# Position bias of a decoder layer: one scratch copy read as reversed, paced skewed blocks

## What is computed

```python
def t5_bucket(dist):
    max_exact = NUM_BUCKETS // 2
    n = jnp.maximum(dist, 0)
    nf = jnp.maximum(n, max_exact).astype(jnp.float32)
    large = max_exact + (jnp.log(nf / max_exact) / math.log(MAX_DISTANCE / max_exact)
                         * (NUM_BUCKETS - max_exact)).astype(jnp.int32)
    large = jnp.minimum(large, NUM_BUCKETS - 1)
    return jnp.where(n < max_exact, n, large)
...
        bias = bias_tab[t5_bucket(t_pos[None, :, None] - sel)]
        logits = logits + jnp.moveaxis(bias, 3, 2)
        logits = jnp.where(valid[:, :, None, :], logits, -jnp.inf)
        p = jax.nn.softmax(logits, axis=-1)
```

## Time and profile before

| | |
|---|---|
| median of 3 runs | 2173.0 us |
| lowest, highest | 2170.37, 2174.82 us |
| span of the profiled execution | 2173.1 us |
| TensorE matmul busy | 2142.9 us, 99% |
| VectorE busy | 1208.3 us, 56% |
| ScalarE busy | 962.8 us, 44% |
| GpSimd busy | 31.4 us, 1% |
| mean HBM rate | 188 GB/s |

### The profile page before, as it was taken

The page is one execution under the profiler, slowest core; times in us unless marked ns, Lnnn a source line. Parts: engine busy times, 40 slices in busy tenths (PEclk is TensorE's granted clock), DMA queues, the critical chain, the costliest instruction groups (busy, mean ns, idle before and its releaser), DMA issues.

```text
span 2173.1 us, 25372 instructions
## 1 busy us (share of the span) xinstructions
PE 2142.9 (99%) x9610; PEld 1769.4 (81%) x9610; DVE 1208.3 (56%) x1419; ACT 962.8 (44%) x1079; POOL 31.4 (1%) x57
## 2 busy tenths in 40 slices
PE   8999999999999999799999999999999999999998
PEld 7888888888888887688888888888888888888887
DVE  5545445444444656699577655465545445444444
ACT  5444444444444453344465444464444444444442
POOL 0000000000000000200000000000000000000000
PEclk9999999999999999899999999999999999999999
DMA  7666666665666566666555566656666666666664
GB/s 233 211 188 189 187 192 189 187 190 187 194 193 193 172 184 169 178 205 185 167 162 181 174 192 209 187 187 199 192 187 190 186 191 190 186 189 194 193 193 151
DMA packets 213607, 408.76 MB, mean 188 GB/s; under 512 B 17361, under 2 KB 17689, under 8 KB 213152
## 3 DMA queue, kind: packets, MB, share of 16 engines
q1 hardware_dynamic: 208752, 399.16, 60.6%
q0 software_dynamic: 4640, 8.59, 1.4%
q10 hardware_dynamic: 144, 0.04, 0.0%
HBM read 404.05 MB, written 3.67 MB: 188 GB/s over the span
## 4 chain that ended last, share of the span: by engine, by line
PE 95%; DMA 3%; DVE 1%; ACT 0%; issue 0%; POOL 0%; DVEq 0%; ACTq 0%; POOLq 0%
PE acc L1171 92%; DMA raw<-in_w_in_dram 2%; PE msc L1207 2%; PE msc L1171 2%; DVE wlo L774 1%; DVE res L806 0%; DVE conv_out L950 0%; DMA res<-in_x_dram 0%; ACT whi L430 0%; ACT act_hi L441 0%; DVE act_lo L818 0%; ACT junk L498 0%; POOL stat L339 0%; PE msc L1367 0%; PE msc L1369 0%
## 5 line engine op out<-in xcount | busy, mean ns | idle before, releaser
L774 DVE TENSOR_TENSOR wlo<-raw,whi 128x1024 fp32r<-128x1024 f32 x756 | 922.3, 1221 | 922.0 <-ACT whi L430 916.7
L430 ACT ACTIVATE whi<-raw 128x1024 fp32r<-128x1024 f32 x756 | 798.0, 1057 | 1143.1 <-PE acc L1171 1090.7
L1171 PE MATMUL acc<-whi,act_hi 128*128 128x512 f32 x2048 | 811.7, 396 | 17.5 <-DVE wlo L774 17.5
L1171 PE MATMUL acc<-whi,act_lo 128*128 128x512 f32 x2048 | 801.2, 391 | 0.0
L1171 PE MATMUL acc<-wlo,act_hi 128*128 128x512 f32 x2048 | 800.8, 391 | 0.0
L1171 PEld LDWEIGHTS acc<-whi,act_hi 128*128 128x128 f32 x2048 | 386.6, 189 | 101.2 <-issue 14.3
L1171 PEld LDWEIGHTS acc<-whi,act_lo 128*128 128x128 f32 x2048 | 386.7, 189 | 81.7
L1171 PEld LDWEIGHTS acc<-wlo,act_hi 128*128 128x128 f32 x2048 | 387.1, 189 | 80.2 <-issue 1.7
L1171 PE MATMUL acc<-whi,h_hi 128*128 128x512 f32 x704 | 274.2, 389 | 0.0
L1171 PE MATMUL acc<-whi,h_lo 128*128 128x512 f32 x704 | 273.9, 389 | 0.0
L1171 PE MATMUL acc<-wlo,h_hi 128*128 128x512 f32 x704 | 273.9, 389 | 0.0
(11 more groups left out here) (160 smaller groups left out, 804.9 us busy)
## 6 DMA issues: line engine op xcount, KB each, us to landing
raw<-in_ffn_wg_dram SPq DMA_DIRECT2D x176, 512.0 KB, 3.6
raw<-in_ffn_wu_dram SPq DMA_DIRECT2D x176, 512.0 KB, 3.6
raw<-in_ffn_wd_dram SPq DMA_DIRECT2D x176, 512.0 KB, 3.7
raw<-in_w_in_dram SPq DMA_DIRECT2D x160, 512.0 KB, 3.6
raw<-in_w_out_dram SPq DMA_DIRECT2D x32, 512.0 KB, 3.6
raw<-in_w_pw_dram SPq DMA_DIRECT2D x16, 512.0 KB, 3.7
raw<-in_w_o_dram SPq DMA_DIRECT2D x16, 512.0 KB, 4.1
res<-in_x_dram SPq DMA_DIRECT2D x4, 512.0 KB, 7.8
```

Source lines behind the costliest of these rows:

```text
L430: nc.scalar.activation(whi[:, j % RING, 0:kts * width], raw[:, j % RING, 0:kts * width], ACT.Copy).then_inc(hi_ready, 1)
L774: nc.vector.tensor_tensor(wlo[:, j % RING, 0:n], raw[:, j % RING, 0:n], whi[:, j % RING, 0:n], ALU.subtract).then_inc(lo_ready, 1)
L1171: return nc.tensor.matmul(o, a, b, **kw)
```

## The change

The scratch tensor holds each head's row once, 8 by 383 values, and is written with one DMA, as soon as the fourth transposed piece has been evicted (`tr_evicted` 4). The 16 reads all start from the same row of their head: row p of a read starts p values further right. For that, the one-hot matrix is built with its columns reversed, and the two reads of a head land in exchanged places of `bias`. VectorE reads `bias` backwards. The reads of head h wait until `mm_done` is at the start of `qk0` plus 4h slabs; the writes have no such wait.

```diff
             pool.wait_ge(tr_evicted, 4)
-            for h in range(0, HEADS, 2):
-                pool.wait_ge(mm_done, MIX["qk0"][0] + 2 * h)
-                pool.dma_start(bias_scratch[h:h + 2], rel_rows[h:h + 2, :].rearrange("h (o r) -> h o r", o=1)
-                               .to_broadcast([2, P, RELS])).then_inc(bias_out, 16)
-            pool.wait_ge(bias_out, 16 * HEADS // 2)
+            pool.dma_start(bias_scratch, rel_rows[:]).then_inc(bias_out, 16)
+            pool.wait_ge(bias_out, 16)
             for h in range(HEADS):
-                skew = bass.AP(bias_scratch.tensor, h * P * RELS + P - 1, [[RELS - 1, P], [1, SEQ]])
-                pool.dma_start(bias[:, h, 0:SEQ], skew).then_inc(bias_full, 16)
-                skew = bass.AP(bias_scratch.tensor, h * P * RELS + 2 * P - 1, [[RELS - 1, P], [1, P]])
-                pool.dma_start(bias[:, h, SEQ:SPAN], skew).then_inc(bias_full, 16)
+                pool.wait_ge(mm_done, MIX["qk0"][0] + 4 * h)
+                skew = bass.AP(bias_scratch.tensor, h * RELS, [[1, P], [1, SEQ]])
+                pool.dma_start(bias[:, h, P:SPAN], skew).then_inc(bias_full, 16)
+                skew = bass.AP(bias_scratch.tensor, h * RELS, [[1, P], [1, P]])
+                pool.dma_start(bias[:, h, 0:P], skew).then_inc(bias_full, 16)
...
-                                                        in1=bias[:, k, :], op0=ALU.mult, op1=ALU.add))
+                                                        in1=bias[:, k, ::-1], op0=ALU.mult, op1=ALU.add))
...
-    n = np.maximum(2 * P - 1 - np.arange(RELS), 0)
+    n = np.maximum(2 * P - 1 - np.arange(RELS)[::-1], 0)
...
-    args.append(nc.dram_tensor("bias_scratch", (HEADS, P, RELS), mybir.dt.float32).ap())
+    args.append(nc.dram_tensor("bias_scratch", (HEADS, RELS), mybir.dt.float32).ap())
```

## The result

| | before | after |
|---|---|---|
| median | 2173.91 us (4 runs, 2170.37 to 2174.89) | 2152.23 us (4 runs, 2151.52 to 2152.44) |
| ratio | | 0.9903, 95% interval 0.9892 to 0.9915 |
| span of the profiled execution | 2173.1 us | 2150.7 us |
| its time | | 2152.44 us |
| mean granted clock | 0.995 | 0.999 |

The changed kernel takes 1.0% less, 21.7 us by the medians and 22.4 us by the spans. The forecast was 2150.1 us in a range of 2147.5 to 2156.7.

A forecast was written before the change was run, and what follows sets the result against it. TensorE's slab products were taken as the bound (92% of the chain), except where slabs come late; 2173.1 - 23.0 (broadcast writes gone) + 0 (single write) + 0 (paced reads) + 0 (backward read) = 2150.1 us, range 2147.5 to 2156.7.

The forecast's parts named there:

- The loss of 23.0 us: Between the transposes behind `qk0` and `qk2`: 62.84 us taken, 39.9 needed; removing the broadcast writes gives -23.0 us.
- Two parts of it, waits and clock: Same stretch: TensorE waits 14.2 us for `wlo`, and a granted clock of 0.86 over 63 us makes 8.8; together 23.0.
- The single write at 0: One 12 KB write of 8 rows, ahead of the gate, costs 0, at most 0.2 us; nearest store lands in 2.2 us.
- The paced reads at 0: The 16 reads, as pairs every 4 slabs (10.9 us), cost 0; 4.6 us if every pair came through to TensorE whole.
- the first rival: Each of the eight paced pairs of reads passes its 0.57 us on to TensorE: 2154.7 us; chance 9%.
- The rivals that had the reads of one shared row slow: Reads as slow as the writes, 2173 us, 2%; or each pair holds the loads for 5.7 us, 2196 us, 4%.
- The backward read at 0: VectorE's 8 backward reads of `bias`, 0.548 us each before, cost 0 on the path; without idle time up to 4.4 us.
- The reserve of 13.0 us: In the disturbed stretch, TensorE loses something only when a slab load takes more than about 13.0 us.
- The price of a write, 5.7 us each: The four old broadcast writes share the loss: 23.0 / 4 = 5.7 us each.
- Why the loads were late: Slab loads wait on a few DMA engines working through the broadcast writes, two engines a write; not bandwidth.
- The sum's base: The sum started from the profiled execution's 2173.1 us, taken as 0.1 us from the median.
- The rival by the page's rate for an engine: At 27 GiB/s an engine the writes land quickly and aren't what holds the loads; the stall stays, 2173 us; 2%.

The follow-up runs named there:

- copies128: Changed kernel plus the four old broadcast writes (two heads, 128 copies, 383 KB each) into an unread scratch, at 0, 4, 8 and 12 slabs of `qk0`; 2175.11 us.
- nopace: Changed kernel without the waits that pace the reads, so all 16 go out back to back after the single write; 2152.47 us.
- copies96: As `copies128`, but with 96 copies in place of 128 in each added write (287 KB); 2164.16 us.
- eight_heads: Changed kernel plus one broadcast write of all eight heads, 128 copies, 1.5 MB, from SBUF into an unread scratch at the start of `qk0`; 2171.4 us.
- hbm2: Changed kernel plus `copies128`'s bytes at the same times, copied from the scratch rows in HBM, two heads outermost, 128 copies inside; 2152.43 us.
- apart: As `copies128`, but the two heads of each added write stand four partitions apart (h and h+4) instead of side by side; 2152.27 us.
- one_head: Changed kernel plus eight broadcast writes of one head each, 128 copies, 192 KB, two at each of `copies128`'s four times; 2185.65 us.

## Why the prediction was right, and where it was not

**The loss of 23.0 us.** Right in size, place and sign: the same stretch of the program now takes 39.92 us, forecast 39.9. It was 0.2 us too large, as its 62.84 took its two ends from two views; within one it is 62.68. `copies128` shows that the writes are enough to bring it all back.

**Two parts of it, waits and clock.** Both parts are there, in `copies128` too. But that 14.2 + 8.8 gave the loss exactly was luck: the same sum gives 26.0 in `copies128`, where 23.6 were lost. The waits are read directly; what is left beside them, 8.6 us before and 7.7 in `copies128`, is the price of the clock.

**The single write at 0.** 3.5 us to landing, not on the path. The 2.2 us of the nearest row was too low; it didn't matter.

**The paced reads at 0.** Right: TensorE has no wait and a clock of 1.00 from 845 to 949 us, so the first rival, pairs that pass on 0.57 us each, isn't seen. `nopace` adds that the pacing brings nothing. The rivals that had the reads of one shared row slow fall with landings of 3.3 to 6.1 us. The last pair went out at 924.1, as worked out, and `bgate` at 925.12.

**The backward read at 0.** 549 against 548 ns. Right, even without its cover.

**The reserve of 13.0 us.** Right as a threshold: 11.9 us costs nothing, 14.9 us does. What a load beyond it costs was not worked out, and turned out steeper than I then expected of `copies96`.

**The price of a write, 5.7 us each.** 6.3 when they stand alone. It is no price of a write as such: the one of `eight_heads` cost 19.2 us.

**Why the loads were late.** Here the step was incomplete. I wrote "not bandwidth, but a few engines working through the writes". That the engines are held is so: from 861 to 866 us of the kernel before, GpSimd's queue takes 23.0% of the time of the 16 engines, 3.7 of them, and the slab loads get 1.2%. That it is because they are few is not. `hbm2` and `apart` keep the two engines and lose nothing; `eight_heads` and `one_head` have eight and 16 and lose 19.2 and 33.4 us. What the step left out is the source: every run that lost 12 us or more wrote out of one group of four partitions at a time, or 1.5 MB at once out of two groups. The forecast came out all the same, because the change removes the whole of these writes. Had the change been to put the two heads four partitions apart, the same reasoning would have forecast no gain, and the runs say 22.8 us (2175.11 to 2152.27).

**The sum's base.** I took the span of 2173.1 us for the whole time of the execution, 0.1 us from the median. Every run with both numbers shows its time 1.7 us above its span (2152.44 and 2150.7), so the base was 2174.8 and the sum 2151.8. That term was 1.7 us off, and explains most of the 2.1 us between forecast and median. By the spans the forecast, 2150.1, stands beside 2150.7. The median of 2152.23 lies 0.1 us above what the prediction gave the forecast alone, 2147.5 to 2152.1, and in the part of the range that was there for the first rival; it is this term that put it there, not the rival.

**The rival by the page's rate for an engine** (writes quick, stall from elsewhere) falls with `copies128`.

## What to carry to other kernels

A small DMA can hold a big stream without using bandwidth: here writes out of one group of partitions held about four engines (3.7), the loads got 1.2% of the engines' time, and all DMA together moved 28 GB/s. Look at the landing times of the stream beside the small DMAs, not at bytes or at the number of engines. Replicate on the read side, where 128 reads of one row in HBM land in 3 to 6 us, and not by writing copies out of one or two partitions. And work out how late a load may be before the bound engine stops: below that, 37 us of ScalarE's waits cost nothing, above it, every copy more cost about 0.36 us.

## What the runs showed of the hardware

- 128 copies read from two neighbouring partitions: 383 KB in 19.2 us; from two partitions four apart 14.6 us; from HBM 14.5 us, again with two rows outermost; from HBM spread wide 5.4 us; from 128 partitions 5.6 us.
- One partition as the source of a DMA on all 16 engines: 0.99 busy at 87 GB/s, and the dearest of all, 33.4 us for 1.5 MB. Here more engines on a narrow source were worse than few: `copies128` lost 22.9 us with the same bytes.
- Reads whose rows start 4 bytes apart in one row of 1.5 KB land in 3.3 to 6.1 us in pairs. Back to back, as before the change, they take 4.0 to 7.3 us with a median of 5.2 (`nopace`), against 3.2 to 5.7 and 4.1 for separate copies; the two bursts stand in different stretches, so whether the shared row is what costs that 1 us is open.
